# A hybrid diffusion layer: half of each Hyena unit's inverse butterflies move from VectorE to GpSimd

## The reference, cut to what matters

```
def long_conv(u, h_fwd, h_bwd, d_skip):
    kern = jnp.concatenate([h_fwd, zeros, jnp.flip(h_bwd[1:], 0)], axis=0)
    spec = jnp.fft.rfft(u, n=2 * l_, axis=1) * jnp.fft.rfft(kern, axis=0)[None]
    y = jnp.fft.irfft(spec, n=2 * l_, axis=1)[:, :l_]
    return y + u * d_skip

z = x1 * long_conv(v, h[:, 0, 0], h[:, 0, 1], d[0])
out = x2 * long_conv(z, h[:, 1, 0], h[:, 1, 1], d[1])
```

## Time and profile before

| | us |
|---|---|
| median of 3 runs | 1743.55 (1738.53 to 1744.39) |
| profiled execution, its own time | 1743.24 |
| its span (first to last instruction) | 1741.4 |
| PE busy in the span | 1540.7 (88%) |
| DVE busy | 1207.1 (69%) |
| ACT busy | 919.7 (53%) |
| POOL busy | 307.9 (18%) |
| granted TensorE clock, mean | 0.946 of full |
| the stage of the change, from VectorE's first instruction to its last | 872.28 to 956.98 |

### The profile page before, as it was taken

One profiled execution on the slowest core, in us unless ns is written; L12 is line 12 of the kernel. 1 busy time (PEld: TensorE's weight loads), 2 busy tenths in 40 slices (PEclk: granted clock), 3 DMA queues, 4 the chain that ended last, 5 costly groups with the idle time before them and its releaser, 6 DMA issues. The chain is left out here.

```text
span 1741.4 us, 21707 instructions
## 1 busy us (share of the span) xinstructions
PE 1540.7 (88%) x8298; PEld 1258.9 (72%) x8298; DVE 1207.1 (69%) x1403; ACT 919.7 (53%) x1308; POOL 307.9 (18%) x371
## 2 busy tenths in 40 slices
PE   6899999988989699998976999199999999999991
PEld 3686788777877589876475787078888888888871
DVE  4872754395655556665798534888888888888873
ACT  5441364375446376543100444167777777777753
POOL 0300500160016685000000443000100010001001
PEclk9999999998998899999988998599999999999996
DMA  9571210050018544211121522389999999999967
GB/s 351 165 263 55 114 49 1 25 168 27 1 41 256 185 113 122 89 32 61 61 97 49 208 96 74 153 341 394 392 376 402 395 389 381 401 396 395 377 216 217
DMA packets 109098, 345.13 MB, mean 198 GB/s; under 512 B 37501, under 2 KB 46998, under 8 KB 84419
## 3 DMA queue, kind: packets, MB, share of 16 engines
q1 hardware_dynamic: 99534, 320.34, 48.6%
q0 software_dynamic: 5328, 18.88, 4.5%
q10 hardware_dynamic: 4133, 4.53, 1.0%
HBM read 301.14 MB, written 37.32 MB: 194 GB/s over the span
## 5 line engine op out<-in xcount | busy, mean ns | idle before, releaser
L3635 DVE TENSOR_TENSOR w_lo<-w_raw,w_hi 128x2048 fp32r<-128x2048 f32 x192 | 438.1, 2291 | 64.1 <-ACT w_hi L3577 64.1
L3577 ACT ACTIVATE w_hi<-w_raw 128x2048 fp32r<-128x2048 f32 x192 | 368.1, 1918 | 142.9 <-PE ps L3522 132.7
L3520 PE MATMUL ps<-w_hi,xsT_hi 128*128 128x512 f32 x512 | 202.1, 395 | 1.1 <-DVE xsT_lo L3640 1.1
L3522 PE MATMUL ps<-w_hi,xsT_lo 128*128 128x512 f32 x512 | 199.8, 390 | 0.0
L3521 PE MATMUL ps<-w_lo,xsT_hi 128*128 128x512 f32 x512 | 199.5, 390 | 0.0
L3488 POOL DMA_INDIRECT moe_sum<-y,idx_col x15 | 30.3, 2021 | 461.0 <-ACT y L3597 430.0
L3520 PEld LDWEIGHTS ps<-w_hi,xsT_hi 128*128 128x128 f32 x512 | 96.2, 188 | 20.6 <-DVE xsT_lo L3640 1.5
L3522 PEld LDWEIGHTS ps<-w_hi,xsT_lo 128*128 128x128 f32 x512 | 96.1, 188 | 20.3
L3521 PEld LDWEIGHTS ps<-w_lo,xsT_hi 128*128 128x128 f32 x512 | 96.2, 188 | 19.3
L3520 PE MATMUL ps<-w_hi,hiddenT_hi 128*128 128x512 f32 x256 | 99.7, 390 | 0.6 <-DVE hiddenT_lo L3652 0.6
L3521 PE MATMUL ps<-w_lo,hiddenT_hi 128*128 128x512 f32 x256 | 99.6, 389 | 0.0
(11 more groups left out here) (610 smaller groups left out, 3612.2 us busy)
## 6 DMA issues: line engine op xcount, KB each, us to landing
w_raw<-in_moe_w_gate SPq DMA_DIRECT2D x64, 1024.0 KB, 6.5
w_raw<-in_moe_w_up SPq DMA_DIRECT2D x64, 1024.0 KB, 8.2
w_raw<-in_moe_w_down SPq DMA_DIRECT2D x64, 1024.0 KB, 8.5
w_mod_row<-in_w_mod SPq DMA_DIRECT2D x32, 512.0 KB, 4.9
w_mod<-in_w_mod SPq DMA_DIRECT2D x8, 1024.0 KB, 17.6
dn_ma<-dn_ma SPq DMA_DIRECT2D x16, 512.0 KB, 4.0
dn_mT<-dn_ma SPq DMA_DIRECT2D x20, 256.0 KB, 3.6
x_tile<-in_x SPq DMA_DIRECT2D x8, 512.0 KB, 16.0
```

Of the source, the lines that this page charges most:

```text
L3520: nc.tensor.matmul(out, h[:, kk, :], wh[w][:, c:c + 512], start=kk == 0, stop=False)
L3522: last = nc.tensor.matmul(out, l[:, kk, :], wh[w][:, c:c + 512], start=False, stop=kk == KD - 1)
L3577: nc.scalar.activation(wh[q % RING][:, :], S.raw[q % RAW][:, :], ACT.Copy).then_inc(s.hi, 1)
L3635: nc.vector.tensor_tensor(wl[q % RING][:, :], S.raw[q % RAW][:, :], wh[q % RING][:, :].bitcast(F32), ALU.subtract).then_inc(s.lo, 1)
```

## The change

GpSimd takes over half of groups E and F. When D of a unit is done, GpSimd computes the difference of the halves of `p1` into a buffer of its own, `pq` (in place of line 3073), waits for that, and writes classes 1 and 3 of `W` (in place of 3078 and 3079), which raises a new semaphore `w_odd`. VectorE keeps the sum and classes 0 and 2, and then raises `w`. Before VectorE overwrites `p1` in the next unit, it waits for GpSimd's subtraction (`pool_pq`). For units of the second convolution GpSimd waits until TensorE's first-convolution products with that `W` are done (`inv`). TensorE takes the classes in the order 0, 2, 1, 3 and waits for `w` ahead of the even and for `w_odd` ahead of the odd ones; the first of the two result banks is so complete after three quarters of an inverse instead of after half.

```diff
@@ -2954,7 +2954,7 @@
     assert low.at <= S.hT_at + KD * D * 4
     S.w_out = Plan(nc, S.hT_at + KD * D * 4, S.stage_at).take("w_out", [P, KD, D])
     plan = Plan(nc, high)
-    with Stage(nc, "hy_d", "tab w_out fwd even odd_half ab x p yc pq w inv z fin") as s:
+    with Stage(nc, "hy_d", "tab w_out fwd even odd_half ab x p yc pq w inv z fin pool_pq w_odd") as s:
         W = plan.take("hy_w", [P, 2, BT, CLASSES, 2, P])
         X = plan.take("hy_x", [P, CLASSES, 2, P])
         p1 = plan.take("hy_p1", [P, CLASSES, 2, P])
@@ -2962,6 +2962,7 @@
         ab = plan.take("hy_ab", [P, 2, 2, P])
         cd = plan.take("hy_cd", [P, 2, 2, P])
         ev = plan.take("hy_odd", [P, 2, 2, P])
+        pq = plan.take("hy_pool_pq", [P, 2, 2, P])
         X8 = X[:, :, :, :].rearrange("p s q c -> p (s q) c")
         UNITS = [(u, u // (2 * BT), u // BT % 2, u % BT) for u in range(4 * BT)]
 
@@ -2994,8 +2995,8 @@
 
             def inverse(u):
                 u, o, g, b = UNITS[u]
-                pe.wait_ge(s.w, u + 1)
-                for r in range(CLASSES):
+                for r in (0, 2, 1, 3):
+                    pe.wait_ge(s.w_odd if r % 2 else s.w, u + 1)
                     bank, at = 4 + 2 * g + r // 2, (r % 2) * 256
                     first, end = b == 0 and r % 2 == 0, b == BT - 1 and r % 2 == 1
                     if o == 0:
@@ -3038,6 +3039,20 @@
                     act.wait_ge(s.ab, u)
                 nc.scalar.activation(ev[:, :, :, :].rearrange("p r q c -> p (r q c)"), S.ps[:, 2 * (u % 2) + 1, :], ACT.Copy
                                      ).then_inc(s.even, 1)
+
+        @s.block.gpsimd
+        def _(pool):
+            for u, o, g, b in UNITS:
+                pool.wait_ge(s.yc, u + 1)
+                if u:
+                    pool.wait_ge(s.w_odd, u)
+                nc.gpsimd.tensor_tensor(pq[:, :, :, :], p1[:, 0:2, :, :], p1[:, 2:4, :, :], ALU.subtract).then_inc(s.pool_pq, 1)
+                pool.wait_ge(s.pool_pq, u + 1)
+                W8 = W[:, g, b, :, :, :].rearrange("p s q c -> p (s q) c")
+                if o:
+                    pool.wait_ge(s.inv, 2 * g + 2)
+                nc.gpsimd.tensor_tensor(W8[:, 2:8:5, :], pq[:, 0, :, :], pq[:, 1, ::-1, :], ALU.add)
+                nc.gpsimd.tensor_tensor(W8[:, 6:2:-3, :], pq[:, 0, :, :], pq[:, 1, ::-1, :], ALU.subtract).then_inc(s.w_odd, 1)
 
         @s.block.vector
         def _(dve):
@@ -3060,6 +3075,8 @@
                 nc.vector.tensor_tensor(X8[:, 2:8:5, :], cd[:, 0, :, :], cd[:, 1, ::-1, :], ALU.subtract)
                 nc.vector.tensor_tensor(X8[:, 6:2:-3, :], cd[:, 0, :, :], cd[:, 1, ::-1, :], ALU.add).then_inc(s.x, 1)
                 dve.wait_ge(s.x, u + 1)
+                if u:
+                    dve.wait_ge(s.pool_pq, u)
                 for p, k in ((p1, kc), (p2, ks)):
                     last = nc.vector.tensor_tensor(p[:, :, :, :], X[:, :, :, :],
                                                    k[:, b, o, :, g * P:(g + 1) * P].unsqueeze(2).to_broadcast([P, CLASSES, 2, P]),
@@ -3069,14 +3086,10 @@
                 nc.vector.tensor_tensor(p1[:, :, 0, :], p1[:, :, 0, :], p2[:, :, 1, :], ALU.subtract)
                 nc.vector.tensor_tensor(p1[:, :, 1, :], p1[:, :, 1, :], p2[:, :, 0, :], ALU.add).then_inc(s.yc, 1)
                 dve.wait_ge(s.yc, u + 1)
-                nc.vector.tensor_tensor(X[:, 0:2, :, :], p1[:, 0:2, :, :], p1[:, 2:4, :, :], ALU.add)
-                nc.vector.tensor_tensor(X[:, 2:4, :, :], p1[:, 0:2, :, :], p1[:, 2:4, :, :], ALU.subtract).then_inc(s.pq, 1)
+                nc.vector.tensor_tensor(X[:, 0:2, :, :], p1[:, 0:2, :, :], p1[:, 2:4, :, :], ALU.add).then_inc(s.pq, 1)
                 dve.wait_ge(s.pq, u + 1)
-                W8 = W[:, g, b, :, :, :].rearrange("p s q c -> p (s q) c")
                 nc.vector.tensor_tensor(W[:, g, b, 0, :, :], X[:, 0, :, :], X[:, 1, :, :], ALU.add)
-                nc.vector.tensor_tensor(W[:, g, b, 2, :, :], X[:, 0, :, :], X[:, 1, :, :], ALU.subtract)
-                nc.vector.tensor_tensor(W8[:, 2:8:5, :], X[:, 2, :, :], X[:, 3, ::-1, :], ALU.add)
-                nc.vector.tensor_tensor(W8[:, 6:2:-3, :], X[:, 2, :, :], X[:, 3, ::-1, :], ALU.subtract).then_inc(s.w, 1)
+                nc.vector.tensor_tensor(W[:, g, b, 2, :, :], X[:, 0, :, :], X[:, 1, :, :], ALU.subtract).then_inc(s.w, 1)
 
             def gated(g):
                 dve.wait_ge(s.inv, 2 * g + 2)
```

## The result

The kernel with the change takes 1748.89 us (median of 20 runs), the kernel before 1744.33 (20 runs beside it): a ratio of 1.0027 [1.0019, 1.0035], or 4.7 us more (3.3 to 6.1). I had said 1741.0 with a range up to 1748.5. The profiled execution took 1746.19, its span 1744.4, 3.0 more than the span before.

A forecast was written before the change was run, and what follows sets the result against it. VectorE was taken to bound the stage. Eight units gaining 0.32 us each, 2.56, less 0.05 at the last inverse, make 2.5 us off the runs' 1743.55: forecast 1741.0 us, range 1736.5 to 1748.5.

The forecast's parts named there:

- What VectorE loses: In each unit, one instruction of E (0.61 us) and half of F (0.67) leave VectorE, together 1.28 us.
- Exclusion, the turns of E, the difference and F's first, A untouched: SBUF work excludes: E ends 0.72 us after D, GpSimd's difference 1.85, F's first 2.13; A, reading PSUM, keeps 0.68.
- rival 1: In the units, GpSimd costs VectorE nothing: -10.3 us, 1733.2; chance 0.08.
- rival 2: VectorE holds on through its wait between E and F, odd classes come late: 0 to -1 us, 1743; chance 0.15.
- rival 4: GpSimd wins the start after D, its difference runs before E: +0.73 a unit, +5.8 us, 1749.4; chance 0.13.
- The second 0.34 later at 2.47: F's second instruction follows the first undisturbed, ending 2.47 us after D; next A starts at 2.39 instead of 2.71.
- rival 3: GpSimd enters between F's two instructions: 0.16 a unit lost, +1.3 us in all, 1744.9; chance 0.14.
- the 0.60 for GpSimd's classes: Behind F, GpSimd's second class takes 0.60 us, done by 3.55 after D, under A, before B starts at 3.70.
- Nothing after the stage is moved against another: Behind the stage, everything keeps its spacing and starts 2.5 us earlier.
- 0.05 at the last inverse: At the stage's end, the first result bank is whole later, so its read delays the second: 0.05 us taken, at most 0.07.
- Unit 4's slack: Time between TensorE finishing unit 4's spectrum and VectorE taking it: 1.35 us before, about 1.0 with the change.
- The odd half waits for nothing: In TensorE's inverse, odd classes come at about 3.55 us after D, wanted at 4.3 or later: 0.8 us to spare.

The follow-up runs named there:

- left_out: The changed kernel with GpSimd's part of every unit left out (odd classes of W stay zero): 1732.34 us, ratio 0.9934 to the kernel before, unit 7.90.
- after_late_classes: The changed kernel, but GpSimd also waits for VectorE's part of W before writing the odd classes: 1742.49 us, ratio 0.9991 to the kernel before.
- the probe parts: Parts of a stage added to the kernel before: a row of VectorE instructions, all operands in SBUF, with GpSimd arriving during it; kept out, GpSimd lasted 4.29 to 4.43 us.
- after_warm: The changed kernel with 10 products of constant tables on TensorE ahead of the last inverse: 1742.81 us, ratio 0.9993 to the kernel before.
- doubled: The kernel before with VectorE's full unit, GpSimd also doing its three instructions into a copy nobody reads: 1761.4 us, ratio 1.0099, unit 11.19.

## Why the prediction was wrong

1. **What VectorE loses: right.** 1.28 a unit; left_out shows 9.17 - 7.90 = 1.27.
2. **Exclusion, the turns of E, the difference and F's first, A untouched: right.** 0.69, 1.70 and 1.37 stand in the rows, A keeps 0.68. Rivals 1, 2 and 4 are out: 3091 shows 1.37, and E doesn't grow.
3. **"The second 0.34 later at 2.47": the step that failed.** It assumed that GpSimd's first class doesn't get in between F's two. It does, in every unit; F's second takes 0.94 and the unit 9.39 instead of 8.85. The forecast gain of 0.32 a unit became a loss of 0.22. That is rival 3, to which I gave 0.14. Its price was a little low too, 0.16: it had GpSimd's class end 0.48 behind F's first, and the rows have 0.58 (880.73 to 881.31) and A 0.53 later than forecast. after_late_classes takes this turn away and has 8.86 where no classes lie under the unit's A. Its other units, at 9.03, show a second term that was too low, though it moved nothing in the changed kernel: the 0.60 for GpSimd's classes, which take 0.72 and don't fit under A as forecast.
4. **Why that step failed.** I took the answer from one row, and of VectorE's instructions that were longer, eight in a row and reading fp32r. Of the probe parts 28 have GpSimd getting in at the next boundary and six keep it out, all six with an fp32r tile read by VectorE's row and an arrival in the last but one instruction, as in the earlier trace rows. F reads f32 and is of the other kind., of F's size, and the earlier trace rows pointed to turns by order of arrival. The Trainium skill, SBUF — State Buffer, section "Who interferes with whom", says that whoever issues first gets the shared pair of ports for the whole instruction. The prediction had weighed that rule with the right consequence (a class between F's two) and set it aside. The unit's rows agree with it (0.94 for F's second); the six parts kept out (4.29 to 4.43) don't, if to have arrived first is to have issued first.
5. **"Nothing after the stage is moved against another", and 0.05 at the last inverse: wrong.** Seven steps lose 1.51 and the last unit 0.17. The stage loses 0.76 more in the last inverse, and the output projection starts 1.2 later still, behind line 233 (3.78 against 2.60). Both are TensorE at or near 1.2 GHz: the granted share is 0.56 in the last inverse and 0.50 in line 233, where it was 0.63 and 0.74. Before, TensorE had run inverse 6 at full clock (3.72) ahead of its long pause; now inverse 6 takes 5.41 and the pause is shorter (5.95 against 7.43). Sum: 1.51 + 0.17 + 0.76 + 1.16 = 3.6 us, the 93.25 - 89.65 above. The forecast had -2.5 there, so it is 6.1 off: 4.2 by the turn in F (1.68 instead of -2.56) and 1.9 by TensorE's clock, for which it had no term: its 0.05 at the last inverse was for the first bank's later read. Rival 3's price had only the units, and so stood at 1744.9. Unit 4's slack, forecast at about 1.0, shrank to 0.33 (its spectrum ends at 910.48, A starts at 910.81), since `inverse(2)` takes 6.57 at a granted 0.56 instead of 5.33 at 0.70. It still held, and cost nothing.
6. **The odd half waits for nothing: right.** The last inverse starts at 951.59, the odd classes are there at 952.11, long before its even half of the 16 rows is through, and after_warm runs all of it in 3.72.
7. **What stays open.** The profiled spans differ by 3.0 us, the medians by 4.7 (3.3 to 6.1); what lies ahead of the stage varies more than that: its first instruction stands between 868.71 and 875.94 in the profiles of these kernels, which are equal up to there. The changed kernel's profiled execution (1746.19) was also 2.7 below its median, that of before 1.1 below its own, so the rows explain 3.6 us and not all of the 4.7. And the clock's share is only partly settled: setting the clock ahead of the last inverse brought about 6 us in the changed kernel, more than the 2.3 its profile shows, and nothing measurable in the two others. Why the granted clock falls where it does was not worked out.

The part of the change that does pay was hidden in the sum. The difference costs 0.35 a unit, since what VectorE saves in E it waits out in F; the classes, placed behind F, run under A for 0.17 a unit at most. Taken apart, the forecast would have found it in its own rows: within a unit A is the only place where VectorE leaves SBUF to GpSimd, and its 1.3 us hold two classes, not three instructions.

## What to carry to other kernels

Work given to GpSimd beside a VectorE that works from SBUF was not parallel here: it cost nearly its own duration (2.02 of 2.2 us in doubled) unless it lay under VectorE instructions with an operand in PSUM, so find that gap first and give GpSimd only what fits, released so that it can't come earlier. For who gets in between two VectorE instructions, assume the one that arrives first, at every boundary; one row that shows otherwise needs the same type, place and length as yours before it may decide. And a bound engine's gain or loss near a stage's end can pass through TensorE's clock, which here added as much again (1.9 us to the 1.7 of the units).

## What the runs showed of the hardware

- GpSimd gets in at VectorE's next boundary, even one that has no wait, in 28 parts of the probes; it is kept out in six, where VectorE's row reads an fp32r tile and only one instruction of it is left (4.29 to 4.43 us instead of 3.2 to 3.3). With f32 alone at the same place it got in, in the one part that had it (3.30).
- A VectorE instruction held up by GpSimd ends 0.28 after GpSimd's, if it is 128x256: F's second here as in the earlier trace rows.
- GpSimd's 128x256 for a class, with a strided output and one input read backwards, takes 0.72, against 0.61 in the earlier trace rows; which of the two costs it was not separated.
- The last inverse's 16 rows take between 3.72 and 6.58 us in these kernels, by the granted clock alone (1.00 to 0.56). Their duration times the granted share is 3.65 to 3.72 in each. Behind table products 0.83 and 1.65 us of idle gave 3.72, 2.26 gave 5.41; but ahead of inverse 6 of the kernel before 3.47 of idle gave 3.72 too, so the pause alone doesn't decide it.
